# Gathering fourteen experts' tokens in two blocks, with expert 1's gate matrix between them

## What is computed

```python
def expert_choice_ffn(h, w_router, w_gate, w_up, w_down):
    B, T, D = h.shape
    cap = CAPACITY_FACTOR * T // N_EXPERTS
    aff = jax.nn.softmax((h @ w_router).astype(jnp.float32), axis=-1)
    g, idx = lax.top_k(jnp.swapaxes(aff, 1, 2), cap)
    xg = jax.vmap(lambda xb, ib: xb[ib])(h, idx)
    a = jnp.einsum('becd,edf->becf', xg, w_gate)
    u = jnp.einsum('becd,edf->becf', xg, w_up)
    y = jnp.einsum('becf,efd->becd', jax.nn.silu(a) * u, w_down) * g[..., None].astype(h.dtype)
    return jax.vmap(lambda yb, ib: jnp.zeros((T, D), yb.dtype).at[ib.reshape(-1)].add(yb.reshape(-1, D)))(y, idx)
```

## Time and profile before

| | us |
|---|---|
| median of 3 runs | 1991.64 |
| lowest, highest run | 1990.75, 1997.35 |
| the profiled execution | 1997.49 |
| its span, first to last instruction | 1995.7 |

### The profile page before, as it was taken

How to read it: one execution, slowest core, us unless ns; L and a number is a source line. 1 busy time by engine, 2 the same in 40 slices (tenths; PEclk the granted TensorE clock), 3 DMA queues, 4 the chain that set the end, 5 groups by cost and what they waited for, 6 DMA issues and landing times.

```text
span 1995.7 us, 22783 instructions
## 1 busy us (share of the span) xinstructions
PE 1786.2 (90%) x9208; PEld 1138.6 (57%) x9208; DVE 632.3 (32%) x1363; ACT 556.9 (28%) x1070; POOL 513.6 (26%) x654
## 2 busy tenths in 40 slices
PE   6999999979899888888889999998999988888787
PEld 3788997879443222222258889887975322222223
DVE  1287344764400000101144853548622000000011
ACT  3444344223421101111144444432333111011011
POOL 0787344246100000000037754424631000000000
PEclk8999999989999999999999999899999999999999
DMA  9535534465799999999973354353465999999996
GB/s 349 126 104 182 192 117 156 130 231 193 297 376 426 427 425 428 427 427 427 426 211 127 106 204 154 109 189 132 169 253 211 404 428 426 426 428 427 427 426 260
DMA packets 123544, 567.78 MB, mean 285 GB/s; under 512 B 21808, under 2 KB 31280, under 8 KB 98352
## 3 DMA queue, kind: packets, MB, share of 16 engines
q1 hardware_dynamic: 112656, 543.91, 68.9%
q10 hardware_dynamic: 9920, 20.84, 2.8%
q0 software_dynamic: 864, 1.58, 0.3%
HBM read 550.57 MB, written 15.73 MB: 284 GB/s over the span
## 4 chain that ended last, share of the span: by engine, by line
PE 54%; DMA 36%; DVE 6%; ACT 2%; SPq 1%; issue 1%; POOL 0%; ACTq 0%; DVEq 0%
PE banks L776 29%; PE banks L1322 11%; DMA work<-in_w_gate 7%; DMA ring<-in_w_up 6%; DMA work<-in_w_up 6%; DMA ring<-in_w_down 6%; DMA ring<-in_w_gate 4%; DMA work<-in_w_down 3%; PE banks L782 2%; DMA ring<-in_w_ada 1%; PE banks L1082 1%; PE banks L1292 1%; PE banks L788 1%; ACT work L1421 1%; DMA work<-gates_spill 1%; ACT hT L1450 1%
## 5 line engine op out<-in xcount | busy, mean ns | idle before, releaser
L717 POOL TENSOR_TENSOR ring_fp32r<-ring,ring_fp32r 128x256 fp32r<-128x256 f32 x592 | 461.3, 812 | 854.9 <-ACT ring_fp32r L1421 854.2
L1322 PE MATMUL banks<-ring,work 128*64 128x512 f32 x1776 | 402.7, 597 | 77.0 <-DMA ring<-in_w_gate 33.5
L776 PE MATMUL banks<-xT_fp32r,ring_fp32r 128*128 128x384 f32 x1280 | 349.9, 346 | 1.8 <-POOL ring_fp32r L717 1.8
L1421 ACT ACTIVATE work<-banks 32x512 f32<-32x512 f32 (+7 forms) x404 | 205.4, 529 | 454.4 <-PE banks L1322 250.8
L1322 PEld LDWEIGHTS banks<-ring,work 128*64 128x64 f32 x1776 | 122.5, 136 | 335.4 <-issue 199.0
L1322 PE MATMUL banks<-work 128*64 128x512 f32 x972 | 225.8, 601 | 40.4 <-DMA work<-in_w_gate 14.9
L776 PEld LDWEIGHTS banks<-xT_fp32r,ring_fp32r 128*128 128x128 f32 x1280 | 237.2, 191 | 14.7 <-issue 7.2
L776 PE MATMUL banks<-hT_fp32r,ring_fp32r 128*128 128x384 f32 x640 | 217.3, 340 | 0.0
L2317 DVE SCALAR_TENSOR_TENSOR xT<-banks,mod,xT 128x128 f32<-128x128 f32 (+1 forms) x128 | 47.1, 413 | 445.5 <-PE banks L1358 445.1
L1421 ACT ACTIVATE ring_fp32r<-ring 128x1024 fp32r<-128x1024 f32 (+1 forms) x164 | 154.5, 969 | 94.1 <-PE banks L776 74.2
L1322 PEld LDWEIGHTS banks<-work 128*64 128x64 f32 x972 | 67.5, 137 | 180.7 <-issue 112.5
(11 more groups left out here) (293 smaller groups left out, 1736.1 us busy)
## 6 DMA issues: line engine op xcount, KB each, us to landing
ring<-in_w_up SPq DMA_DIRECT2D x38, 2048.0 KB, 30.6
ring<-in_w_gate SPq DMA_DIRECT2D x37, 2048.0 KB, 30.6
ring<-in_w_down SPq DMA_DIRECT2D x36, 2048.0 KB, 30.1
ring<-in_w_in SPq DMA_DIRECT2D x28, 2048.0 KB, 8.3
ring<-in_w_ada SPq DMA_DIRECT2D x24, 2048.0 KB, 8.4
work<-in_w_down SPq DMA_DIRECT2D x20, 2048.0 KB, 30.6
work<-in_w_gate SPq DMA_DIRECT2D x18, 2048.0 KB, 30.6
work<-in_w_up SPq DMA_DIRECT2D x16, 2048.0 KB, 30.6
```

What stands on the lines that cost most here:

```text
L717: ins = pool.tensor_tensor(rounded(w_), w_, rounded(hi_), ALU.subtract)
L776: mm = pe.matmul(dst, a_, b_, start=(first and i == 0), stop=(last and i == 2))
L1322: mm = pe.matmul(dst[64 * hf:64 * hf + 64, :], x(k), w[kk][:, 512 * hf:512 * hf + 512], start=(k == 0), stop=(k == KC - 1), tile_position= ...
L1421: return act.activation(dst, src, ACT.Copy, scale=scale)
```

## The change

The first matrix of expert 1, its gate matrix a1, is multiplied after the first eight of the sixteen gather units, and no longer behind the transposes of the tables.

```diff
                 for q in range(16):
                     if q >= 4:
                         pe.wait_ge(sem["xg_evac"], 18 * l + 2 + q - 3)
+                    if q == 8:
+                        expert_a(1)
                     gather(PS[:, 4 + q % 4, 0:448], q, 2, NE).then_inc(sem["xg_out"], 1)
                 pe.wait_ge(sem["xg_evac"], 18 * (l + 1))
                 pe.wait_ge(sem["selg_ready"], l + 1)
...
                 for e in range(1, NE):
                     units = COMBINED.get(e, ())
-                    expert_a(e)
+                    if e >= 2:
+                        expert_a(e)
                     if units:
                         combine_early(units[0])
                     if e == 1:
```

## The result

| | us |
|---|---|
| median with the change, 4 runs | 2005.49 (2003.01 to 2007.95) |
| median of the kernel before, 4 runs on the same chip | 1991.20 (1989.82 to 1997.35) |
| ratio | 1.0074, interval 1.0049 to 1.0098 |
| profiled execution of the change | 2004.82, span 2003.0 |

The change costs 14.3 us by the medians, and between 9.8 and 19.5 us by the interval of the ratio. 2005.7 was forecast, with 14.0 us as the sum.

A forecast was written before the change was run, and what follows sets the result against it. The weight stream at 427 GB/s was taken to bound the expert stages. Delaying load 10 by a1 costs 2 x 7.02 = 14.0 us, other terms nothing: 1991.64 + 14.0 = 2005.7 us, range 2002 to 2012.

The forecast's parts named there:

- The stream sets the pace, and its end follows its restart: Expert stages: weight loads at 427 GB/s bound them; whatever moves load 10's issue moves the end, about 427 us later.
- Price of a1 ahead of `sgt_out`: Gather in both layers: a1 delays the table transposes, hence load 10, by its full 7.02 us; 14.0 us in all.
- Loads 11 and 12 queued early gain nothing: Stream restart: a1's slots free early, but both loads stand behind load 10; gain 0 to 1.24 us per layer, taken as nothing.
- The split gather for nothing: Gather in two blocks around a1: costs 0 to 0.63 us per layer for a second evacuation wait; taken as 0.
- The new wait in front of d0 is covered: Before d0: without a1's cover TensorE is 2.2 us later, but queued loads 10 to 12 cover it; price nothing.
- the dear rival: Wait in front of d0 also on the path: 14.0 + 4.5 = 18.5 us, 2010.1; chance 0.05.
- The times of issue: Signs on SP and TensorE: load 10 issued about 581.5 and 1561.6, first TensorE wait for a load ahead of 642.
- The first rival: Pause around the gather: loads 11 and 12, in early slots, fill it; 8.3 us gained, 1983.3; chance 0.03.
- The second rival: Expert stages: the stream catches up, only the 2.2 us before d0 count; 4.5 us dearer, 1996.1; chance 0.06.

The follow-up runs named there:

- 1: Against the kernel before, only the first half of a1 moved into the middle of the gather; second half left in place: 2000.14 us against 1993.84, ratio 1.0041.
- 4: The kernel before, TensorE's order untouched, with loads 10 and 11 in a1's slots and load 12 in the seventh: 1998.98 us, ratio 1.0030 to the kernel before.
- 3: The change, TensorE's order kept, with loads 10 and 11 in a1's slots and load 12 in the seventh: 1994.77 us against 1993.84 before, ratio 1.0004.
- Number 5: The change, slots kept, with the bare wait in front of d0 removed by edits on TensorE, ScalarE and VectorE: 2004.40 us, ratio 1.0060 to the kernel before.
- 6: The change with both edits, the slot order of 3 and the removed d0 wait of Number 5: 1986.09 us against 1991.72 before, ratio 0.9976.
- 7: Kernel 1 (half of a1 ahead), with load 10 in that half's slot and load 11 in the seventh: 1987.21 us against 1991.72 before, ratio 0.9971.
- 8: Kernel 6, with table transposes waiting only for the gather units whose banks they write: 1985.64 us against 1991.45 before, ratio 0.9964.

## Why the prediction was right

- *The stream sets the pace, and its end follows its restart.* Restart to last landing was 427.88 and 427.40 us against 427.25 and 427.78. Shown by experiment as well: half of a1 ahead costs about half (1), a later restart costs as much when a change of slots alone brings it about (4: 6.0 us, 7 expected), and nearly all of the cost goes by a change of slots alone (3). That the cost by the medians came within 0.3 us of the sum is luck, since its interval runs from 9.8 to 19.5 us; the 14.7 us up to the last landing are the better measure of the sum.
- *Price of a1 ahead of `sgt_out`, 2 x 7.02 us.* Measured 7.32 us in layer 0 from a0 to load 10. The same distance in layer 1 grew by 34.96 - 29.53 = 5.43, but there the first half of a0 had run slowly before (5.35 us, 3.65 now), so 7.13 without those 1.70 us.
- *Loads 11 and 12 queued early gain nothing.* 246 GB/s against 251 in the restart: so taking nothing for it was right. The Trainium skill's page "DMA: Bandwidth & Descriptors" (Anatomy of one DMA) gives a fixed cost of about 2.0 us per transfer, on another issue path; the estimate from it put the low end of the sum at 10.0 us, and the traces show no such gain from loads queued together.
- *The split gather for nothing* was the one term of the sum a little off: 0.3 us in layer 0, within the bounds of 0 and 0.63.
- *The new wait in front of d0 is covered.* From a0 to d0 it is 38.74 us where it was 35.99, or 2.75 later, 0.3 of it from the split; 2.2 was worked out. The clock did fall, as the dear rival had it: d0's first half took 5.31 us, or 1.66 more, beside the 2.75. Load 13 came 4.4 us later behind load 6 than before, and was still early. The time alone would not exclude the dear rival's 18.5 us. Number 5 does: it shows that this lag costs nothing that can be measured, and number 3 that it is on the path once fewer loads cover it.
- *The times of issue.* Load 10 of layer 1 was expected near 1561.6 and came at 1555.31, since the mixing stage of that execution was 6 us shorter; mainly for the same reason the profiled execution took 2004.82 us and not 2011.5. TensorE's first wait for a load came at 640.32, ahead of 642.18, as expected, and 2.4 us sooner when counted from a0:

```profile
640.32 3.65 PE L1322 MATMUL banks<-work 128*64 128x512 f32 x16 [1.04 <-DMA work<-in_w_up]
```

- *The first rival*, the early slots, was refuted by SP's rows, and right about the possibility: once the order of slots lets these loads pass, the cost goes (3), and with d0's wait covered as well the kernel is faster than before (6, 7, 8). In numbers 6 and 8 the gain is 5 to 7 us by the ratio, but only 3.3 and 4.9 of the 8.3 us of lost stream, and 2.5 at the last landings.
- *The second rival*, a stream that catches up, would have cost 4.5 us; the interval begins at 9.8, and the stream stayed at 427 GB/s.

## What to carry to other kernels

Where a stream of loads sets the pace, look at what the next load waits for, on the queue that issues it, before moving work between matmul groups: whatever is put ahead of that one signal delays every load behind it by its full length, however well it fills a gap elsewhere. A buffer freed early is worth nothing while the queue's head waits for another buffer, so the order of buffers has to follow the order in which they come free. And a load keeps a stream going only if it is issued early enough before the stream runs dry: here 0.2 and 0.6 us ahead were too late (6), and 1.8 us were enough.

## What was not expected

A load of 2 MB that is issued 0.2 us before the stream runs dry does not prevent the dip of a restart: 240 GB/s over 3 us in number 6, 246 and 251 after real pauses; with 0.6 us ahead the dip is a little shallower (292). And three loads queued at once restart no faster than one (246 against 251 GB/s).

The clock of TensorE fell to its lower level behind the bare wait. The granted clock of the change in layer 0, half a microsecond within d0's first half, columns as in the earlier trace rows:

```profile
587.00:587.50 0.50, 0.50 (x4) 0.23 (x2) 0.00 (x0) 0.00 (x0) 0.00 (x0) 0.50 1.07 459
```

0.50 of full speed is the 1.2 GHz level. Ahead of it TensorE had been idle for 2.40 us, busy for 0.72 and idle for 0.69; in before, with 0.69 us alone at the same place, the half matrix took 3.65 us and not 5.31. What decides it is not shown: behind idle times of 0.64 and 0.75 us a0's first half took 5.35 us in layer 1 of before, and 3.65 us behind 0.63 and 0.75 us in layer 1 of the change.
